# One burst of late modulation products per round in place of two, in the attention stage of a hybrid encoder layer

## What is computed

```
mod = silu(c) @ w_ada + b_ada          # 6 vectors of 1024 per sequence, w_ada is 1024 x 6144
sh1, sc1, g1, sh2, sc2, g2 = split(mod)
h = rmsnorm(x) * (1 + sc1) + sh1
proj = h @ w_in                        # A: q,k,v   B: q,k,v   two gates
A = differential attention, 8 heads, each with two softmax maps; rmsnorm of its output
B = stick-breaking attention, 16 heads
x += g1 * ((sig(gate_A) * (A @ w_oa) + sig(gate_B) * (B @ w_ob)) @ w_out)
x += g2 * mixture_of_experts(rmsnorm(x) * (1 + sc2) + sh2)
```

## Time and profile before

| | |
|---|---|
| median of 3 runs | 824.5 us (823.54 to 825.18) |
| span of the profiled execution, first to last instruction | 826.1 us |
| TensorE's granted clock, mean | 0.952 |
| PE busy | 712.6 us (86%), 5345 records |
| DVE, ACT, POOL busy | 352.1, 271.2, 94.7 us |
| moved by transfers | 199.17 MB |
| rounds 3 to 10 of stage A | from 84 to 229 us |

### The profile page before, as it was taken

One profiled execution on the slowest core, in us unless ns is written; L12 is line 12 of the kernel. 1 busy time (PEld: TensorE's weight loads), 2 busy tenths in 40 slices (PEclk: granted clock), 3 DMA queues, 4 the chain that ended last, 5 costly groups with the idle time before them and its releaser, 6 DMA issues.

```text
span 826.1 us, 13819 instructions
## 1 busy us (share of the span) xinstructions
PE 712.6 (86%) x5345; PEld 576.6 (70%) x5345; DVE 352.1 (43%) x552; ACT 271.2 (33%) x500; POOL 94.7 (11%) x158
## 2 busy tenths in 40 slices
PE   0698899999899999999988999878999898788770
PEld 0387788888789999999977999755565444454430
DVE  1555666666425433334423356642323232223225
ACT  0444555554354444455434442300111011011010
POOL 2012222222000001000110000011011001000011
PEclk9899999999999999999998999878999999999995
DMA  9957277765734886442215437789799999999915
GB/s 325 332 152 221 80 209 210 211 191 180 241 118 132 212 261 168 128 112 78 80 31 164 144 116 293 273 363 350 304 418 417 417 418 418 418 417 419 377 55 190
DMA packets 131176, 199.17 MB, mean 241 GB/s; under 512 B 11688, under 2 KB 113464, under 8 KB 117816
## 3 DMA queue, kind: packets, MB, share of 16 engines
q1 hardware_dynamic: 123032, 185.63, 63.7%
q0 software_dynamic: 6208, 11.02, 3.9%
q10 hardware_dynamic: 1888, 1.86, 0.7%
HBM read 193.47 MB, written 16.55 MB: 254 GB/s over the span
## 4 chain that ended last, share of the span: by engine, by line
PE 51%; DMA 17%; ACT 8%; DVE 8%; issue 6%; SPq 4%; ACTq 2%; DVEq 2%; POOL 1%; POOLq 0%
PE ps L575 24%; DMA e_w<-in_w 14%; PE ps L570 8%; PE ps L572 8%; PE ps L571 7%; ACT w_hi L1122 4%; SPq L507 3%; DVE w_lo L1435 2%; DMA vec_rows<-in_norm_g 1%; DVE w_lo L1443 1%; DMA yb<-expert_rows 1%; SPq L512 1%; ACT sig_r L1239 1%; PE ps L999 1%; ACT z_na L1285 1%
## 5 line engine op out<-in xcount | busy, mean ns | idle before, releaser
L575 PE MATMUL ps<-e_w,xgT 128*64 128x256 f32 x1024 | 125.6, 403 | 29.5 <-issue 17.8
L575 PEld LDWEIGHTS ps<-e_w,xgT 128*64 128x64 f32 x1024 | 81.7, 145 | 69.1 <-issue 24.4
L570 PE MATMUL ps<-hT_hi,w_hi 128*128 128x320 f32 x320 | 102.3, 320 | 4.4 <-DVE w_lo L1435 4.2
L1435 DVE TENSOR_TENSOR w_lo<-raw,w_hi 128x2048 fp32r<-128x2048 f32 (+1 forms) x26 | 68.1, 2619 | 82.6 <-ACT w_hi L1122 82.6
L572 PE MATMUL ps<-hT_hi,w_lo 128*128 128x320 f32 x320 | 99.6, 311 | 0.0
L571 PE MATMUL ps<-hT_lo,w_hi 128*128 128x320 f32 x320 | 99.4, 311 | 0.0
L1767 DVE TENSOR_SCALAR h_s<-h_e 128x256 f32<-128x256 f32 x16 | 4.7, 294 | 155.9 <-ACT h_e L1352 155.9
L570 PEld LDWEIGHTS ps<-hT_hi,w_hi 128*128 128x128 f32 x320 | 60.7, 190 | 7.2 <-issue 4.1
L1122 ACT ACTIVATE w_hi<-raw 128x2048 fp32r<-128x2048 f32 (+1 forms) x26 | 56.4, 2168 | 21.7 <-PE ps L572 21.7
L571 PEld LDWEIGHTS ps<-hT_lo,w_hi 128*128 128x128 f32 x320 | 60.8, 190 | 0.0
L572 PEld LDWEIGHTS ps<-hT_hi,w_lo 128*128 128x128 f32 x320 | 60.7, 190 | 0.0
(11 more groups left out here) (260 smaller groups left out, 1293.8 us busy)
## 6 DMA issues: line engine op xcount, KB each, us to landing
e_w<-in_w SPq DMA_DIRECT2D x96, 1024.0 KB, 23.4
raw<-in_w_in SPq DMA_DIRECT2D x45, 512.0 KB
ada_late<-in_w_ada SPq DMA_DIRECT2D x16, 1024.0 KB, 5.2
ada_first<-in_w_ada SPq DMA_DIRECT2D x8, 1024.0 KB, 21.3
raw<-in_w_in SPq DMA_DIRECT2D x8, 1024.0 KB
raw<-in_w_oa SPq DMA_DIRECT2D x4, 1024.0 KB
raw<-in_w_ob SPq DMA_DIRECT2D x4, 1024.0 KB
raw<-in_w_out SPq DMA_DIRECT2D x4, 1024.0 KB
```

The source lines that it names most:

```text
L570: nc.tensor.matmul(out, lhs_hi, rhs_hi, start=first, stop=False, skip_group_check=True)
L575: return nc.tensor.matmul(out, lhs, rhs, start=first, stop=last, skip_group_check=True)
L1435: V.tensor_tensor(w_lo[j][:, :, 0:width], raw[j][:, :, 0:width], f32(w_hi[j][:, :, 0:width]), ALU.subtract).then_inc(split_done, 1)
```

## The change

In rounds 3 to 10 the first burst, and the waits in front of it, are taken away from behind the value products. Both chunks are multiplied in one burst behind the transposes of the normalized output, where the second burst stood: for each k, four matmuls go to the four column groups, two from each chunk. The burst waits for both chunks and for what the first burst waited for. `late_used` is raised twice, by the last matmul of either chunk, so both raises come at the end of the burst. The helper `ada` goes.

```
-            def ada(buf, out, done):
-                n = ADA_COLS // len(out)
-                for k in range(KD):
-                    for m in range(len(out)):
-                        last = mm(out[m], c_cols[:, k, :], buf[:, k, m * n:(m + 1) * n], k == 0, k == KD - 1)
-                last.then_inc(done, 1)
...
-            def ada_chunk(h, n):
-                pe.wait_ge(late_in[n], 16 * (h - 2))
-                ada(ada_late[n], [ps[32 * b:32 * b + 32, ADA_BANK, 384:512] for b in (2 * n, 2 * n + 1)], late_used)
+            def ada_round(h):
+                for n in range(2):
+                    pe.wait_ge(late_in[n], 16 * (h - 2))
+                for k in range(KD):
+                    for b in range(4):
+                        last = mm(ps[32 * b:32 * b + 32, ADA_BANK, 384:512], c_cols[:, k, :],
+                                  ada_late[b // 2][:, k, b % 2 * P:(b % 2 + 1) * P], k == 0, k == KD - 1)
+                        if k == KD - 1 and b % 2:
+                            last.then_inc(late_used, 1)
...
                     last.then_inc(a_pv, 1)
-                    pe.wait_ge(a_staged, min(3 * h, 24) if isinstance(h, int) else 3 * h)
-                    if not (isinstance(h, int) and h == 3):
-                        pe.wait_ge(late_out, l)
-                    ada_chunk(h, 0)
...
                     last.then_inc(a_oT, 1)
-                    ada_chunk(h, 1)
+                    pe.wait_ge(a_staged, min(3 * h, 24) if isinstance(h, int) else 3 * h)
+                    if not (isinstance(h, int) and h == 3):
+                        pe.wait_ge(late_out, l)
+                    ada_round(h)
```

## The result

The changed kernel takes 830.16 us (median of 6 runs, 828.78 to 832.78) against 824.95 us for the kernel before on the same chip: a ratio of 1.0061, 95% interval 1.0041 to 1.0080. It is slower by some 5 us, where 2.1 us faster was forecast, and lies above the forecast range.

What follows compares the result with a forecast made beforehand. PE was taken to bound rounds 4 to 7, the softmax chain rounds 9 and 10. Terms -1.87 (round 3), -0.10 (4 to 6), -0.51 (7), +0.34 (into 8), 0 (8 to 10) summed to -2.14: 822.4 us, range 819.0 to 826.0.

Steps and rivals of the forecast that it cites:

- the price of the chunk on SP's queue: Weights and store wait behind one chunk more, delaying ACT's copy in rounds 4 to 6 by 2.75 us.
- Rounds 8 to 10: 0: In the last three rounds PE waits anyway, so removing the first burst gains nothing and costs nothing.
- forecast -1.87: Round 3 gains the whole removed first burst, 1.87 us, since its store is sent before any late chunk is renewed.
- the joint burst is as long as an old one: The 64-record burst behind the output transposes takes 1.87 us, as long as one old burst of 32 records.
- The rival of a longer burst: The joint burst over four groups takes longer, seven times on the path; at 2.80 us, 828.9 us total; chance 0.12.
- the upper bound: Highest price of the extra chunk on SP's queue: 3.1 us, 1 MB at 335 GB/s.
- The lower bound: Lowest price of the extra chunk on SP's queue: 2.5 us, the first pair's late chunk taking 7.7 against 5.2.
- The cover of 2.57 us: Before the change, ACT's wait for the store is hidden by 2.57 us, counted to PE's output transposes.
- That the store wouldn't be held up: Rival: only the rotary step limits rounds 3 to 7, 18.64 us each instead of 20.17; total 816.8 us; chance 0.14.
- 18.30 us: PE's time through round 7 from its key transposes, after a wait of 1.36 us in front of them.
- The 0.22 given to falls of the clock: Rival: the granted clock falls under 1.00 from round 8 on; chance 0.22.
- the forecast's 1.6: The profiled execution's span, 826.1 us, was read as 1.6 us above the median of the runs.

Runs made afterwards that it cites:

- experiment 1: The kernel before, both bursts in place; SP only sends the first chunk later, together with the second: 830.89 us, ratio 1.0076 to the kernel before.
- experiment 2: The changed kernel with SP's order turned, weights and store issued ahead of the two chunks: 824.49 us, ratio 0.9986 to the kernel before.
- experiment 9: The kernel before with the bursts joined behind the output transposes in rounds 8 to 10 alone: 828.78 us, ratio 1.0055.
- experiment 11: The kernel before with the bursts joined behind the output transposes in round 10 alone: 826.81 us, ratio 1.0018.
- experiment 4: The changed kernel with the joint burst behind the value products, none behind the output transposes: 820.34 us, ratio 0.9943 to the kernel before.
- experiment 7: The kernel before, both bursts in place, with SP sending weights and store ahead of the chunks: 824.41 us, ratio 0.9996.
- experiment 6: Experiment 4 with DVE computing `oT_lo` ahead of the sample's softmax combine in rounds 3 to 8: 819.33 us, ratio 0.9937 to the kernel before.
- experiment 8: Experiment 6 with ACT computing `oT_hi` ahead of its copy of the sample's tile 0: 820.39 us, ratio 0.9954 to the kernel before.
- experiment 10: Experiment 6 with the second chunk's half-burst moved behind the output transposes in rounds 9 and 10: 820.14 us, ratio 0.9946 to the kernel before.

## Why the forecast was wrong, step by step

Three steps failed: the price of the chunk on SP's queue was too low, a wait of PE (for `oT_lo`) was put at nothing, and "Rounds 8 to 10: 0" left out what the first burst did in round 10. Counted from the end of one burst to the end of the next:

| round | before, us | forecast, us | measured, us |
|---|---|---|---|
| 4 | 20.17 | 20.16 | 21.13 |
| 5 | 20.17 | 20.35 | 21.18 |
| 6 | 20.16 | 19.89 | 20.48 |
| 7 | 20.17 | 19.66 | 19.97 |
| 8 | 20.50 | 20.84 | 21.81 |
| 9 | 13.69 | 13.69 | 13.71 |
| 10 | 10.90 | 10.90 | 12.06 |

With round 3 (forecast -1.87, measured -1.86) the forecast's -2.14 becomes +2.72 us, an error of 4.86.

- **What was removed, and that the joint burst is as long as an old one: right.** 1.95 us: four column groups with their weight loads fitted into the time of two (64 records in 1.95 us, 32 in 1.94). The rival of a longer burst falls.
- **The chunk's price, "I take 2.75": mis-sized.** The copies of rounds 4 and 5 start 15.54 and 15.59 us after the end of the burst. Counted in the same way it was 11.95 and 12.14 before (12.02 and 12.21 from the start of the key transposes), so they are 3.6 and 3.45 later; the upper bound had been 3.1. (The lower bound was misread as well: the first pair of chunks landed 5.3 and 7.4 us after issue, which gives 2.1; the 7.7 is a later chunk's.) The bounds came from one transfer beside another; here the weights were held up behind both chunks, 6.67 us of issue, and the store behind the weights. This and 0.13 us more from the copy to the end of the burst (5.59; the forecast's 5.39 ends at the next key transposes, 0.07 earlier) make 0.97 + 0.83 = 1.80 of the error. The mechanism, late store, late copy, PE idle at the output transposes, is what the forecast said, and experiments 1 and 2 show it; but PE idles there in rounds 4 and 5 alone, 1.7 us together and not 2 a round, since the waits ahead of it, at the key transposes, had already taken their share. The cover of 2.57 us, too, was counted to the output transposes alone: through the rotary step, 142.96 - 141.75 = 1.21 us was left, and in experiments 9 and 11, where the store is late too, PE waits at the key transposes and nowhere else in rounds 4 to 7. That the store wouldn't be held up is refuted; even with that wait gone (experiments 2 and 4) a round takes 19.6 us and not that rival's 18.64.
- **The missed wait.** The forecast let PE run from the key transposes through the round in 18.30 us, with one wait in front of them. But the second four transposes (L734) wait for `oT_lo`, which hangs on a chain of its own: `o_n`, the maxima, the sample's exponentials, `oT_hi`, `oT_lo`. They stand 1.28 us behind the first four in place of 0.49. No late store is needed for it: with the store ahead of the chunks it is 0.49 with two bursts a round (experiment 7) and 1.28 with one (2). PE's part of the round got shorter and the chain didn't. That 0.79, with 0.14 more on the way to the burst's end, gives round 6 as 1.25 + 18.30 + 0.79 + 0.14 = 20.48, round 7 as 0.76 + 18.30 + 0.79 + 0.14 = 19.99, and makes most of round 8's 0.97: 0.59 + 0.31 + 0.97 = 1.87 of the error. The forecast had put this term at nothing. The burst's place doesn't help: with the joint burst in front (experiment 4) the distance is 1.28 as well.
- **"Rounds 8 to 10: 0": wrong for round 10.** That the first burst gains nothing there was right. It also has a use: without it the holes of 1.8 to 2.4 us appear, and in the trace two stretches of half clock fall into rounds 9 and 10 where there was one, and round 10 is 1.16 us longer. The 0.22 given to falls of the clock, and their place in the upper end of the range, were the author's estimate: no run had shown what a fall costs, and in the table above it is some 1.2 us in rounds 9 and 10. They came at the end of round 9 and in round 10, where the forecast saw a chain with slack, and not from round 8 on. Experiment 9 shows that these rounds alone make the kernel measurably slower.
- **What stays open.** The steps account for +2.7 us, the medians differ by 5.2, the profiled spans by only 1.3. Part of this is the choice of the executions. Wherever a run's time and span are both known, the time is 1.7 to 1.8 us longer, so the trace of before shows an execution of about 827.9 us, 2.9 above its median (the forecast's 1.6 compared a span with a time), and that of the changed kernel one 0.9 below its own. In the trace of before the work ahead of round 2's key transposes took 1.6 us less than in the other, and the stages behind round 10 took 3.0 more, of which 1.5 is a stretch of half clock at 449.5 us that the trace of the changed kernel hasn't. Over all runs the mean granted clock of the changed kernel was 0.945 to 0.953 (mean 0.949), that of before 0.947 to 0.962 (mean 0.955) in the 117 runs beside the experiments. In these the time rises by 0.43 us for each 0.001 of clock that is missing. By that slope the lower clock goes with 2.7 us of the changed kernel's loss, and with 1.8 of experiment 9's 4 (0.952 against 0.957): estimates from runs on several chips, in which the longer round 10 is contained. That half-clock stretches in executions without a trace are the cause is argued from this, not shown.

The fastest kernels are those with the joint burst at the first place (experiments 4, 6, 8 and 10): 0.5 to 0.6% under the kernel before, by measures that don't differ among themselves. Of these, experiment 4 is the simplest.

## What to carry to other kernels

When a transfer is sent by the end of a piece of work, moving that work moves the transfer to another place in its queue: cost everything behind it there, and what waits for that, before counting the instructions saved; here the later place of one transfer alone cost 4.9 us (experiment 1). When a piece is taken off the engine that sets the pace, ask of every wait in its round by how much it was hidden, not only of the first that comes to mind: here three came out, at the output transposes, the rotary step and `oT_lo`, and with the store in time again only the first went away (experiment 2). And the burst that filled a forced wait in round 9 cost nothing, so removing it there gained nothing (13.69 us with it, 13.71 without); done in rounds 8 to 10 together it lost 0.5% (experiment 9).

## What the hardware showed that was not expected

- Four column groups of 32 columns, 64 records of 128 columns, each with a weight load of its own, ran in 1.95 us, two groups with 32 records and 32 loads in 1.94.
- Three weight transfers of 512 KB took 4.33 us to issue behind one chunk of 1 MB, 6.67 us behind two, and 2.18 us with none just ahead of them (experiment 7, at 115.25): what stood ahead on SP's queue held the next transfers up at the issue, and not only in the landing.
- What a stretch of half clock costs depended on what PE was waited for. One of 3.4 us made about 1.2 us in rounds 9 and 10 of the kernels in the table; 6.8 us of it in experiment 6 left these rounds only 0.54 us longer than in experiment 10, which had none.
